# VectorE's order in the FoX heads and their prologue: output product and query's low part ahead of the next key strip's weights, the values' weights ahead of the norm

## What is computed

```python
def fox_shared_kv(h, kv_norm_g, w_kv, b_forget):
    proj = rmsnorm(h, kv_norm_g) @ w_kv
    k, v, f_logit = jnp.split(proj, [D_INNER, 2 * D_INNER], axis=-1)
    ...
    log_f = jax.nn.log_sigmoid((f_logit + b_forget).astype(jnp.float32))
    cum = jnp.cumsum(log_f, axis=1).transpose(0, 2, 1)
    return k, v, cum

def fox_layer(h, norm_g, w_in, w_out, k, v, cum):
    q, r = jnp.split(rmsnorm(h, norm_g) @ w_in, 2, axis=-1)
    ...
        s = jnp.einsum('bhqd,bhkd->bhqk', q[:, :, start:end], k[:, :, :end]).astype(jnp.float32)
        s = s + cum[:, :, start:end, None] - cum[:, :, None, :end]
        ...
        p = jax.nn.softmax(jnp.where(causal, s, NEG_INF), axis=-1)
        outs.append(jnp.einsum('bhqk,bhkd->bhqd', p.astype(v.dtype), v[:, :, :end]))
    ...
    return h + (o * jax.nn.silu(r)) @ w_out
```

## Time and profile before

| | us |
|---|---|
| median of three executions | 1015.65 |
| lowest, highest | 1015.36, 1015.8 |
| the profiled execution's own time | 1015.43 |
| its span in the trace | 1013.6 |
| TensorE's matmuls busy | 1001.2 |
| VectorE busy | 705.2 |
| ScalarE busy | 539.2 |
| GpSimd busy | 50.0 |

### The profile page before, as it was taken

One profiled execution on the slowest core, in us unless ns is written; L12 is line 12 of the kernel. 1 busy time (PEld: TensorE's weight loads), 2 busy tenths in 40 slices (PEclk: granted clock), 3 DMA queues, 4 the chain that ended last, 5 costly groups with the idle time before them and its releaser, 6 DMA issues.

```text
span 1013.6 us, 18909 instructions
## 1 busy us (share of the span) xinstructions
PE 1001.2 (99%) x7699; PEld 937.9 (93%) x7699; DVE 705.2 (70%) x1162; ACT 539.2 (53%) x900; POOL 50.0 (5%) x73
## 2 busy tenths in 40 slices
PE   9999999999999999999999999999999999999998
PEld 8999999999999999997889989999899989888887
DVE  6875677577567784336999976998589876875332
ACT  6754654564464554225475655566366645674332
POOL 0000000000000000000131100001010101100000
PEclk9999999999999999999999999999999999999999
DMA  8221221221122114332333543444234433743412
GB/s 289 78 70 63 81 87 43 83 84 64 63 84 84 64 42 130 132 104 74 126 86 101 110 132 86 104 102 153 83 101 110 118 115 111 237 109 110 154 48 83
DMA packets 40375, 104.00 MB, mean 103 GB/s; under 512 B 4560, under 2 KB 12624, under 8 KB 40288
## 3 DMA queue, kind: packets, MB, share of 16 engines
q1 hardware_dynamic: 39568, 102.11, 33.1%
q10 hardware_dynamic: 720, 0.68, 0.2%
HBM read 94.94 MB, written 7.64 MB: 101 GB/s over the span
## 4 chain that ended last, share of the span: by engine, by line
PE 86%; DVE 7%; issue 3%; ACT 3%; DMA 0%; DVEq 0%; SPq 0%; ACTq 0%
PE psum L1854 57%; PE psum L2149 7%; PE psum L2230 7%; PE psum L1979 2%; PE psum L2208 2%; PE psum L2189 1%; PE psum L1927 1%; PE psum L2176 1%; DVE sq L1128 1%; PE psum L1975 1%; PE psum L2178 1%; PE psum L2177 1%; DVE a_lo L1128 1%; DVE w_lo L1114 1%; PE psum L1948 1%
## 5 line engine op out<-in xcount | busy, mean ns | idle before, releaser
L1114 DVE TENSOR_TENSOR w_lo<-raw,w_hi 128x1024 fp32r<-128x1024 f32 x155 | 190.3, 1246 | 35.0 <-ACT w_hi L612 32.9
L612 ACT ACTIVATE w_hi<-raw 128x1024 fp32r<-128x1024 f32 x155 | 161.6, 1051 | 32.5 <-PE psum L2149 29.5
L1854 PE MATMUL psum<-xh,w_hi 128*128 128x264 f32 x768 | 159.2, 288 | 0.5 <-DVE w_lo L1128 0.3
L1854 PE MATMUL psum<-xl,w_hi 128*128 128x264 f32 x768 | 155.9, 285 | 0.0
L1854 PE MATMUL psum<-xh,w_lo 128*128 128x264 f32 x768 | 155.3, 283 | 0.0
L1854 PEld LDWEIGHTS psum<-xh,w_hi 128*128 128x128 f32 x768 | 118.6, 189 | 2.0 <-issue 1.5
L1854 PEld LDWEIGHTS psum<-xl,w_hi 128*128 128x128 f32 x768 | 119.5, 188 | 0.0
L1854 PEld LDWEIGHTS psum<-xh,w_lo 128*128 128x128 f32 x768 | 119.1, 189 | 0.0
L1854 PE MATMUL psum<-y_lo,w_hi 128*128 128x264 f32 (+2 forms) x400 | 104.8, 314 | 0.0
L575 POOL TENSOR_TENSOR sub<-sub,cst 128x128 f32<-128x128 f32 x64 | 42.2, 661 | 838.2 <-DMA sub<-sums 838.1
L1854 PEld LDWEIGHTS psum<-y_lo,w_hi 128*128 128x128 f32 x400 | 66.7, 188 | 4.6
(11 more groups left out here) (323 smaller groups left out, 2371.9 us busy)
## 6 DMA issues: line engine op xcount, KB each, us to landing
raw<-w_all SPq DMA_DIRECT2D x143, 512.0 KB, 3.4
sub<-sums SPq DMA_DIRECT2D x16, 264.0 KB, 7.5
y_keep<-sq SPq DMA_DIRECT2D x13, 256.0 KB, 2.2
y<-y_keep SPq DMA_DIRECT2D x13, 256.0 KB, 6.1
sub<-sums SPq DMA_DIRECT2D x16, 200.0 KB, 6.4
sub<-sums SPq DMA_DIRECT2D x16, 136.0 KB, 4.9
hT<-xT SPq DMA_DIRECT2D x8, 264.0 KB, 5.8
h_keep<-hT SPq DMA_DIRECT2D x8, 256.0 KB, 4.1
```

Source lines behind the costliest of these rows:

```text
L612: nc.scalar.activation(w_hi[:, n % HI_RING, :], raw[:, n % LO_RING, :], ACT.Copy).then_inc(hi_made, 1)
L1114: nc.vector.tensor_tensor(w_lo[:, n % LO_RING, :], raw[:, n % LO_RING, :], w_hi[:, n % HI_RING, :].bitcast(F32), ALU.subtract).then_inc(lo ...
L1854: i = nc.tensor.matmul(o, w[a][:, k % KT, :], x[b][:, k, c0:c1], start=k == first and a == b == 0, stop=k == last and a == 1)
```

## The change

No instruction is added, dropped or resized. On VectorE, in the rounds whose next head is a Strassen head: `keys_lo` moves from between the sums to ahead of `probs_lo`; where h does not end a group, `fox_out` moves to the front and the low part of the next key weights to behind `summed_queries_lo`; where h ends a group, `fox_out` and `summed_queries_lo` change places. In the prologue, on VectorE: the low part of u02 and the two copies into `rtok` and the gate's minimum move ahead of `fox_key(0)` and `norm(0)`, and `norm(1)` moves behind the gate's cumulated sum and the low part of u03. On ScalarE: the gate's abs, exp and ln move to the front, then the first key's high part, then the first half of `x2h`, then u03's high part, then the second half of `x2h`.

```diff
--- before.py
+++ after.py
@@ -960,15 +960,16 @@
                                      ACT.Copy).then_inc(f_copied, 1)
             end_groups_out(0)
             split_to("u02")
-            act.wait_ge(x2_normed, 1)
-            nc.scalar.activation(x2h[:, 0:4, :], x2n[:, 0:4, :], ACT.Copy).then_inc(x2h_made, 1)
             act.wait_ge(f_logit, 1)
             nc.scalar.activation(f_t, fb, ACT.Abs, bias=vec[0:H, B_F:B_F + 1]).then_inc(f_act, 1)
             act.wait_ge(f_act, 1)
             nc.scalar.activation(f_t, f_t, ACT.Exp, scale=-1.0).then_inc(f_act, 1)
-            keys_hi(0)
             act.wait_ge(f_act, 2)
             nc.scalar.activation(f_t, f_t, ACT.Ln, bias=1.0).then_inc(f_act, 1)
+            keys_hi(0)
+            act.wait_ge(x2_normed, 1)
+            nc.scalar.activation(x2h[:, 0:4, :], x2n[:, 0:4, :], ACT.Copy).then_inc(x2h_made, 1)
+            split_to("u03")
             act.wait_ge(x2_normed, 2)
             nc.scalar.activation(x2h[:, 4:8, :], x2n[:, 4:8, :], ACT.Copy).then_inc(x2h_made, 1)
             split_to("k1")
@@ -1638,23 +1639,23 @@
             split_to("u01")
             dve.wait_ge(f_sum, 3)
             tt(fb, fb, rstd[0:H, :], ALU.mult, f_logit)
-            fox_key(0)
-            norm(0)
-            dve.wait_ge(f_logit, 1)
-            dve.wait_ge(f_act, 1)
-            nc.vector.tensor_scalar(fb, fb, vec[0:H, B_F:B_F + 1], 0.0, ALU.add, ALU.min).then_inc(f_min, 1)
             split_to("u02")
             x = slot("m0") + 1
             dve.wait_ge(rtok_done, 1)
             nc.vector.tensor_copy(rtok[:, 0:NBLK], bank(x, ROOT_AT, ROOT_AT + NBLK * 32).rearrange("p (b n) -> p b n", n=32)[:, :, 0]).then_inc(rtok_made, 1)
             nc.vector.tensor_copy(rtok[0:META, NBLK:NBLK + 1], bank(x, ROOT_AT + 128, ROOT_AT + 129, 0, META)).then_inc(rtok_made, 1)
-            norm(1)
+            dve.wait_ge(f_logit, 1)
+            dve.wait_ge(f_act, 1)
+            nc.vector.tensor_scalar(fb, fb, vec[0:H, B_F:B_F + 1], 0.0, ALU.add, ALU.min).then_inc(f_min, 1)
+            fox_key(0)
+            norm(0)
             dve.wait_ge(f_act, 3)
             dve.wait_ge(f_min, 1)
             tt(f_t, fb, f_t, ALU.subtract, f_log)
             dve.wait_ge(f_log, 1)
             nc.vector.tensor_tensor_scan(fb, ones[0:H, 0:1].to_broadcast([H, T]), f_t, 0.0, ALU.mult, ALU.add).then_inc(f_cum, 1)
             split_to("u03")
+            norm(1)
             split_to("k1")
             norm_lo(0)
             end_values_sum(0)
@@ -1692,19 +1693,19 @@
                     fox_key(n)
                     split_to(f"q{n}")
                     split_to(f"e{n}")
+                    keys_lo(n)
                     probs_lo(h)
                     first_sums(n)
-                    keys_lo(n)
                     second_sums(n)
                     if g is None:
+                        fox_out(h)
+                        summed_queries_lo(n)
                         split_to(f"k{n + 1}")
-                        summed_queries_lo(n)
-                        fox_out(h)
                         if strassen(h + 2):
                             weight_sums(h + 2)
                     else:
+                        fox_out(h)
                         summed_queries_lo(n)
-                        fox_out(h)
                         done(dve, f"m{g}")
                         split_to(f"u{g}0")
                         end_values_sum(g)
```

## The result

The changed kernel took 1018.44 us (median of 7 runs, 1017.63 to 1018.91), the kernel before 1015.49 us beside it (7 runs, 1015.02 to 1015.91). The ratio is 1.003, with a 95% interval from 1.002 to 1.004: slower by about 3 us. As a change that is +2.95 us, where +2.0 was forecast. The profiled execution of after took 1018.44 with a span of 1016.6, 3.0 over the span of before.

A forecast was written before the change was run, and what follows sets the result against it. TensorE was taken as the bound, busy 1001.2 of 1013.6 us. Heads +2.4, ninth step -0.1 and prologue -0.3 gave +2.0, so 1017.7 us on the 1015.65 median; range 1013.6 to 1019.2.

The forecast's parts named there:

- The loop: Ordinary heads: VectorE waits for the attention sum, delaying splits and middle products; 22.52 us a head instead of 22.22.
- The new wait: TensorE's middle products wait for the second weight split, near 0.75 us in seven or eight heads.
- The term of the heads, 2.4: Eight steps from one ordinary head to the next, each longer because the loop closes: +2.4 us in all.
- The scores' wait of 0.1: Ordinary heads: the scores' wait for the output product or query's low part falls from 0.55 to 0.10 us.
- The ninth step, -0.1: Head 12 into 13, without weight sums: part of the scores' wait comes free, -0.1 us.
- The prologue, -0.3 between -0.7 and +0.4: Prologue: 2.6 us won early end in the transposes' wait; a shorter GpSimd hold leaves -0.3 us.
- the step on the hold: Prologue: GpSimd's first weight sum comes sooner, freeing up to 1.1 us of VectorE's held split, at most 0.7 counted.
- the last of the prediction's own signs of being wrong: Forecast is wrong if the prologue's VectorE path is not the one that ends last at the first transposes.
- The bound of +0.4: Prologue's upper bound: one more meeting with GpSimd between 487 and 505 us lengthens a split, costing 0.3.
- No new wait: Rival, heads: scores' wait shrinks 0.4 in nine steps and middle products are not late; 1011.8 us, chance 0.15.
- Today's length: Rival, heads: the loop closes but splits meet no GpSimd work, 22.25 a head; 1015.4 us, chance 0.25.
- both worse: Rival: one more GpSimd meeting in each head and +0.4 in the prologue; 1020.5 us, chance 0.08.

The follow-up runs named there:

- c2: The heads' part of the change alone, plus two unused memsets on VectorE ahead of the weight sums in eight heads: 1019.0 us.
- a3: The kernel before with one move only, the key's low part ahead of the probabilities' low part: 1010.79 us, ratio 0.9953.
- a4: The heads' part of the change, prologue as before, with the key weights' split put back ahead of the output product: 1014.34 us, ratio 0.999.
- d1: a4 with the scores' wait on the query's low part made the last of four instead of the second: 1011.96 us, ratio 0.9967.
- a2: The kernel before with only the prologue's part of the change, heads as before: 1016.45 us, ratio 1.0009.
- a1: The kernel before with only the heads' part of the change, prologue as before: 1018.13 us, ratio 1.0026.
- b1: The prologue's part of the change alone, with GpSimd's first weight sums moved behind its masks of head 1: 1014.97 us, ratio 0.9997.

## Why the prediction came out as it did

The median of 1018.44 lies 0.7 over the forecast of 1017.7. As a change it is further off, 2.95 against 2.0: the kernel before came out 0.16 lower in the measurement beside it. The interval of the ratio, 1.002 to 1.004, times 1015.49 is 1017.5 to 1019.6 and holds the forecast. That the sum comes so near is partly luck. In the traces the heads are 0.6 over their term and the prologue 0.9 over its own, and 0.4 of that is taken back by two differences that have nothing to do with the change as forecast, the 0.3 at the start and the 0.1 in the other steps.

- **The loop: right.** VectorE idle ahead of sq (1.4 forecast, 1.59 found), the split behind it, no gap to the second splits, the middle products as what is late next, in eight heads. Length of a step 22.52 forecast, 22.53 in four of eight and 180.0 / 8 = 22.50 in the mean. The release 0.25 after L2210 was 661.73 - 661.47 = 0.26. c2 shows that the loop is closed, a3 and a4 that the place of the split closes it. With the rows of after the loop's sum is 0.26 + 0.61 + 0.60 + 1.13 + 13.51 + 0.06 + 6.37 = 22.54, the step 5>6 of the table. The new wait was put at 0.75 and is 0.47 in the row above, 0.6 at most. By these rows it is less because the scores lost 0.2 more than forecast (below), which brings TensorE to it later; the two together are set by the loop.
- **The term of the heads, 2.4: under-sized by 0.6.** The failed number is not the loop but what it was subtracted from. One step of before, 22.22, was taken from head 5 to 6, which is the longest of the eight; their mean is 22.13. 8 x (22.50 - 22.13) = 3.0. A difference of 0.3 in a step of 22 wants a mean of all steps, not one row.
- **The scores' wait of 0.1: wrong, without a price.** They start 663.38, and the matmuls before them end their run at 662.94 with a pitch of 0.12: a loss of 0.3, not 0.1. 0.15 from the end of fq_lo to the scores was taken from a row in which another semaphore came last. It is 0.36 when the query's wait is last to be met but not last in the code (662.34 + 0.68 = 663.02 to 663.38; a4, d1). In after it is off the loop, which runs through VectorE and ends in a wait of TensorE of 0.47, and so costs nothing by these rows; in a4 the same 0.21 costs 2 us, since there the loop is through the scores.
- **The ninth step, -0.1: right** (19.34 to 19.23).
- **The prologue, -0.3 between -0.7 and +0.4: wrong sign, and just out of its bounds** (+0.57 in after, +0.84 in a2). The first half of the working holds closely: 2.64 us won by 490 (2.6 forecast), a wait at q0 (0.7 in the list, 0.9 with the refill, 0.8 forecast), 1.55 left at the first scores (1.2 forecast; the wait of 0.4 at r0 didn't come), all of it gone by the transposes, in a wait of 0.5 for the held split (L1855 <- w_lo, in the list) and the 1.3 for pr. What failed is the step on the hold: "up to 1.1 us of that hold go". GpSimd did come sooner, at 506.06 instead of 507.99, as forecast, but VectorE did not stand clear of it. The first sum held the scaled norm product (L1628, 506.39, 2.31 instead of 1.22), the second sum the split (508.62, 2.32). Before had two holds as well, but the earlier trace rows has only the first of the four sums, and the working counted one. The one at the split of the earlier trace rows stayed; the other went from a later split, for which ScalarE does not wait, to L1628, for which it does: t_hi starts at 508.73 instead of 508.23, though after is 0.3 ahead from the start, and so the exps end later and with them the transposes (+0.10 in the delay table) and the gate (+0.59), for which TensorE waits another 0.4. The last exp's sum is read out at 517.25 in after and VectorE takes it up at 517.28, so ScalarE is now what ends last at the transposes, where in before VectorE was (516.75 and 517.47): the last of the prediction's own signs of being wrong has come true for this part. The bound of +0.4 priced a second meeting at 0.3, by the splits of the earlier trace rows, while the row for the hold itself was 1.1. The low bound took "ScalarE is no sooner" into account, the high one did not ask whether ScalarE could be later. The Trainium skill (SBUF — State Buffer, Who interferes with whom) says that the exclusion holds for instructions of VectorE with two inputs in SBUF; the trace agrees, and by that rule L1628 was as open to it as the split (2.31 and 2.32).
- **The rivals.** "No new wait" fell: it needed VectorE's path under 12.8 us, and it is 677.58 - 664.07 = 13.51 in after, as in before. a3, which takes the scores' wait away without the new one, came within 1.0 of this rival's price (1010.8 against 1011.8); that nearness is no support for it, since a3 leaves out the prologue and two of the three moves. "Today's length" is seen in single steps (22.27) only. In "both worse" both parts lose, and both did, but its meeting more in each head came in two of eight, and the time is 2.1 under its price.

Open: why the count of meetings with GpSimd differs between heads and runs, and the 1 us by which c2 is less above a1 in the medians than in the traces.

## What to carry to other kernels

In these runs, on an engine that runs in order, moving an instruction forward was worth something only where it went into idle time (a3); an instruction that waits, put ahead of ready work, turns that work's time into idle time, and whatever is chained behind it is late by it. Add up the chain behind the moved wait until it meets the other engine, and compare it with the time in hand there, over all steps, before asking how long the awaited instruction was waited for. And where a path is freed from a stall, ask what the engines that shared it will meet next: a hold of about 1 us can move, with the GpSimd work 2 us sooner, onto an instruction that another engine waits for.

## What the runs showed of the chip that I had not expected

- The order of several waits ahead of one matmul costs time: 0.36 us from the end of the last awaited instruction to the matmul's start with two waits listed behind its own, 0.15 with its own listed last, and 2.4 us in the run (a4 and d1).
- A SCALAR_TENSOR_TENSOR of VectorE over 128x1024 with both inputs in SBUF is lengthened by a TENSOR_TENSOR of GpSimd as a TENSOR_TENSOR is, 2.31 against 1.22 us, and back to 1.22 when GpSimd's is gone (after, b1).
- The GpSimd instruction is lengthened too: the second sum took 2.16 in after and 2.17 in before, where a sum of the same shape took 1.29 beside no such instruction (in before the fourth, which itself held a split). Which of the two is lengthened went by which was first: in before GpSimd's by 0.12 us (1.36 for the sum, 2.33 for the split), in a3 VectorE's by 0.01 us (2.37 for the sum, 1.22 for the split). So 0.1 us of scatter ahead of such a pair can decide 1.1 us on one engine or the other; this is one trace of a3.
